# A decoder step with gathered experts: a row's weights and diagonal made on ScalarE instead of VectorE, routing in fifteen parts, queries further ahead

## The chip, the cores and the metric

The kernel runs on one core of a Trainium2 chip. The metric is the device time of one execution in microseconds; the time before is 1787.45 us, the median of three runs (1787.36, 1787.45 and 1790.5).

## The reference, cut to what matters

Two layers work on 288 tokens (256 of a prompt, 32 of a sample group), 1024 wide, all in float32. Each layer has a dense token mixer (a chunked gating MLP in layer 0, a short convolution in layer 1) and then an expert mixer that picks 16 of 16,384 experts for each token and each of 8 heads:

```python
q = (xb @ w_query).reshape(PEER_BLOCK, PEER_HEADS, 2, D_HALF)
s = jnp.einsum('thpd,hpkd->thpk', q, sub_keys)          # scores against 2 x 128 keys
sv, si = lax.top_k(s, TOPK_HALF)                        # 16 best of each half
cand = sv[:, :, 0, :, None] + sv[:, :, 1, None, :]      # 256 sums
cv, ci = lax.top_k(cand.reshape(..., 256), TOPK)        # 16 best sums -> expert indices
...
g = jax.nn.softmax(cv, axis=-1)
u_sel = expert_u[idx]
a = jax.nn.gelu(jnp.einsum('thkd,td->thk', u_sel, xb))  # one number for each picked expert
return jnp.einsum('thk,thkd->td', g * a, expert_v[idx]) # weighted sum of their rows
```

The two expert tables stand side by side in memory, so that one picked expert is one contiguous row of 8 KB: 4 KB of `u` and 4 KB of `v`.

## The kernel before, in words

**Items and turns.** The tokens lie in three tiles: two of 128 prompt tokens and one of the 32 sample tokens, which is spread over 128 partitions with two heads on each quarter. One item is one picked expert for each of the 128 partitions: 128 items for each prompt tile and 32 for the sample tile, so 288 for a layer and 576 in all (`ITEMS`). An item is one gather by GpSimd (L628) of 128 rows, 1.05 MB, into one of eight slots of a ring (`uvring`, `RING = 8`).

The engines run through the items in turns, one item a turn. In turn p VectorE makes the dot product of item p with the tokens (`dot`, L1221). ScalarE makes its gelu (`gelu`, L932). VectorE, in turn p+1 and so after the dot product of item p+1, multiplies gelu, softmax weight and a constant pattern of two stacked identities into a 128x64 block (`weigh`, L1232, written to `diag`; 128x32 for the sample tile, L667 on TensorE). TensorE, also in turn p+1, multiplies that block with the `v` half of the slot and sums it in PSUM (`weigh` of TensorE, L675: 8 instructions for an item). Only then is the slot free: GpSimd waits for TensorE's count `v_tensor` to pass item n-8 before it issues gather n. For the first item of a tile TensorE does items n and n+1 together in turn n+2, since the sum of the tile before has to be read out first.

**The planner.** All other work, the dense mixers, norms, queries, scores and routing of the tile to come, is spread over the same turns by a planner that runs when the kernel is built (`plan_steps`). Each step has an engine, an estimated cost and the steps it needs (`mixer_steps`, `route_steps`). In each turn every engine gets a budget (`ROOM`: in the first tile 1.3 us on VectorE, 2.0 on ScalarE and TensorE) and takes steps in order while its credit lasts. A step may follow one of another engine one turn later, and some two turns after TensorE (`slow`). What is planned for turn -1 (`ahead`) runs before the first item. In each turn an engine first does its part for the item, then its planned steps; TensorE does the planned steps first.

**Routing.** The top-16 search of two heads is nine parts of VectorE steps (`route`, parts 0 to 8). Part 0 finds the best eight scores and their places, part 1 strikes them out and finds the next eight and their places, and so on; part 5 hands the scores to ScalarE's exp, part 8 writes the gather's indices and raises `routed`, for which GpSimd waits. The planner puts parts apart by the turns that are left until they are due (`due`, ten turns before the item), and hurries them where few are left.

**The start.** Turn -1 holds the mixer of tile 0, its queries up to the eighth block, the scores of the first four heads and the routing of the first head. The query weights lie in chunks of 1 MB (two blocks each), some of them in the ring's slots: slot 4 holds the chunk of blocks 8 and 9, slot 7 that of blocks 10 and 11, and a gather into such a slot waits until TensorE has used the chunk (`wait_unused`, in L628's queue).

Of the kernel before, what the change touches and what calls it, by code (L numbers as in the profile page):

```python
# [13 lines left out]
P = 128  # L14
# [105 lines left out]
def mixer_steps(n):  # L120
# [90 lines left out]
    for b in range(HP):  # L211
        out.append(("PE", ("q", n, b), blk, [("xT read", l, "ffn", tiles[-1], 1)]))
        out.append(("ACT", ("q read", n, b), 0.35, [("q", n, b)]))
        for b0, count in scores_of(l, tiles[0]):
            if b0 + count - 1 == b:
# [3 lines left out]
                            [("s", l, tiles[0], b0, count)] + ([("route", *scanned, 1)] if scanned else [])))  # L219
    if 2 in tiles:  # L220
        out.append(("PE", ("s", l, 2, 0, HP), 2.0, [("q read", n, HP - 1)]))
        out.append(("ACT", ("s read", l, 2, 0, HP), 0.6, [("s", l, 2, 0, HP)] + [("route", 0, 2, 0, 1)] * l))
    return out


def route_steps(l, t, i):
    n = dict(calls_of(l, t))[i]
    out = [("DVE", ("route", l, t, i, 0), 0.65 * n, [("s read", *scores_for(l, t, i)[1:])])]
    out += [("DVE", ("route", l, t, i, part), 0.65 * n, []) for part in range(1, 9)]
    out += [("ACT", ("exp", l, t, i), 1.8, [("route", l, t, i, 5)]),  # L230
            ("DVE", ("recip", l, t, i), 0.5, [("exp", l, t, i)])]
    return out
# [17 lines left out]
def group_of(k):  # L250
# [7 lines left out]
    (0, 0): {"DVE": 1.3, "ACT": 2.0, "PE": 2.0},  # L258
# [13 lines left out]
def plan_steps():  # L272
# [7 lines left out]
    cut = [k for _, k, _, _ in first].index(("s read", 0, 0, 4, 4)) + 1  # L280
    ahead = first[:cut] + route_steps(0, 0, 0)
# [34 lines left out]
    while any(q for e in ENGINES for q in queues[e]):  # L316
        room = ROOM[ITEMS[p][:2]] if p < len(ITEMS) else {e: 1000.0 for e in ENGINES}
        for e in ENGINES:
            credit[e] = min(credit[e], 0.0) + room[e]
            plan[e][p] = []  # L320
            while True:
                mine = [q for q in queues[e] if q and ready(e, q[0][1], q[0][3], p)]
                hurry = False
                if e == "DVE" and mine and mine[-1][0][1][0] == "route":
# [17 lines left out]
                if hurry and due(k) - p > 8 - k[4]:  # L342
                    break
# [19 lines left out]
ROUTES = [k[1:4] for k in planned("DVE", ("route",)) if k[4] == 8]  # L363
# [60 lines left out]
def trunk(nc, x_tok, w_chunks, rows, ln_gain, ln_bias, w_s, b_s, conv_w, conv_state, sub_keys,  # L424
          expert_uv, ident_c, iota_c, fold_c, tril_c, smask_c,
          y_tok, v_rows, conv_prompt, conv_sample):
    with ExitStack() as ctx:
# [40 lines left out]
        a_gelu = sb("a_gelu", [P, 2 * TOPK])  # L468
        diag = sb("diag", [P, DIAGS, 64])
# [61 lines left out]
        dotted, gelu_done = sem("dotted"), sem("gelu_done")  # L531
# [102 lines left out]
        def _(pe):  # L634
# [203 lines left out]
            for p in range(-1, TURNS):  # L838
# [4 lines left out]
                for n in (p - 2, p - 1):  # L843
                    if 0 <= n < len(ITEMS) and (n in ITEM0.values()) == (n == p - 2):
# [3 lines left out]
        def _(act):  # L848
# [80 lines left out]
            def gelu(n):  # L929
                act.wait_ge(dotted, n + 1)  # L930
                c = n % (2 * TOPK)
                nc.scalar.activation(a_gelu[:, c:c + 1], a_raw[:, c:c + 1], ACT.Gelu_apprx_tanh).then_inc(gelu_done, 1)  # L932

# [19 lines left out]
            for p in range(TURNS):  # L953
                if p < len(ITEMS):
                    gelu(p)
# [378 lines left out]
```

## Time and profile before

| | |
|---|---|
| median of three runs | 1787.45 us |
| the profiled execution | 1791.12 us, of which the span is 1789.3 us |
| busy in the span | TensorE 1346.1 us, VectorE 1219.4 us, GpSimd 672.8 us, ScalarE 286.5 us |
| moved by DMA | 720.95 MB, 604.02 of them by the 576 gathers; 403 GB/s over the span |
| largest groups | VectorE dot L1221 705.4 us (576 of 1225 ns), TensorE L675 687.2 us, VectorE block L1232 158.9 us (512 of 310 ns), ScalarE gelu L932 116.4 us (576 of 203 ns) |

Engines are called PE (TensorE matmul), PEld (TensorE weight load), DVE (VectorE), ACT (ScalarE), POOL (GpSimd) and SP in the rows. The windows view gives for a stretch of time the busy time of each engine, the granted clock of TensorE as a share of full speed, the mean busy share of the 16 DMA engines, and the rate. In a timeline the bracket behind a row is the idle time of that engine before it and what ended it.

### The profile page before, as it was taken

The numbers are of one execution on the slowest core, as the hardware profiler recorded it, in microseconds if no ns is written. First come the engines' busy times: TensorE is split into PE (matmuls) and PEld (weight loads), VectorE is DVE, ScalarE is ACT, GpSimd is POOL, SyncE is SP. The second block draws the span as 40 slices with busy tenths as digits, with TensorE's granted clock in tenths as the row PEclk, the third lists the DMA queues.
The fourth block names the chain that finished last, engine by engine and source line by source line (L and its number), as shares of the span: only waits on it lengthen the run. The fifth ranks groups of instructions, "written<-read, shape, count | busy, mean of one in ns | idle before, by whom it ended". The sixth has DMA issues, their size and how long they took to land.

```text
span 1789.3 us, 22966 instructions
## 1 busy us (share of the span) xinstructions
PE 1346.1 (75%) x8372; PEld 648.1 (36%) x8372; DVE 1219.4 (68%) x3205; ACT 286.5 (16%) x972; POOL 672.8 (38%) x580
## 2 busy tenths in 40 slices
PE   8987999997896877877664598878786666667643
PEld 7973555542563543541110165324441111111100
DVE  1349867755675766756787876766678877775565
ACT  1112130101122101211021120013112011010011
POOL 0013333234332433434445444434344444444452
PEclk9998999998998998887655599888896766766655
DMA  9949999999999999999999999999999999999995
GB/s 394 387 185 381 384 397 420 421 421 422 421 420 421 418 421 415 411 420 421 419 411 403 398 398 421 422 420 421 421 407 421 413 419 415 411 422 419 421 414 244
DMA packets 101185, 720.95 MB, mean 403 GB/s; under 512 B 12080, under 2 KB 12720, under 8 KB 13872
## 3 DMA queue, kind: packets, MB, share of 16 engines
q0 software_dynamic: 82944, 604.02, 81.9%
q1 hardware_dynamic: 17712, 114.87, 15.6%
q8 instruction: 66, 1.08, 0.2%
q10 hardware_dynamic: 416, 0.60, 0.1%
q14 instruction: 47, 0.39, 0.1%
HBM read 717.93 MB, written 1.52 MB: 402 GB/s over the span
## 4 chain that ended last, share of the span: by engine, by line
DMA 54%; PE 27%; DVE 8%; issue 6%; DVEq 2%; POOL 1%; ACT 0%; SPq 0%; POOLq 0%
DMA uvring<-expert_uv_dram,idx 53%; PE psum L675 10%; PE psum L686 7%; PE psum L804 3%; PE psum L718 3%; DVE uvring L1221 2%; DVE diag L1232 1%; POOL uvring L628 1%; DVEq L1008 1%; DVEq L1016 1%; PE psum L694 1%; PE psum L757 1%; PE psum L667 1%; PE psum L825 1%; DVE ti L1021 1%
## 5 line engine op out<-in xcount | busy, mean ns | idle before, releaser
L628 POOL DMA_INDIRECT uvring<-expert_uv_dram,idx x576 | 672.6, 1168 | 1091.3 <-PE psum L675 836.8
L1221 DVE SCALAR_TENSOR_TENSOR uvring<-uvring,xn 128x1024 f32<-128x1024 f32 x576 | 705.4, 1225 | 446.6 <-DMA uvring<-expert_uv_dram,idx 437.2
L675 PE MATMUL psum<-uvring,diag 64*64 64x512 f32 x4096 | 687.2, 765 | 324.1 <-DVE diag L1232 316.3
L675 PEld LDWEIGHTS psum<-uvring,diag 64*64 64x64 f32 x4096 | 130.6, 154 | 742.8 <-DVE diag L1232 671.7
L932 ACT ACTIVATE a_gelu<-a_raw 128x1 f32<-128x1 f32 x576 | 116.4, 203 | 1348.9 <-DVE uvring L1221 1348.3
L686 PEld LDWEIGHTS psum<-xT,wring 128*128 128x128 f32 x1600 | 216.4, 198 | 72.9 <-issue 64.1
L686 PE MATMUL psum<-xT,wring 128*128 128x160 f32 (+1 forms) x1600 | 236.3, 303 | 3.2 <-DMA wring<-w_chunks_dram 3.2
L1232 DVE TENSOR_SCALAR diag<-twin,a_gelu,gate 128x64 f32<-128x64 f32 x512 | 158.9, 310 | 6.0 <-ACT a_gelu L932 6.0
L667 PE MATMUL psum<-uvring,diag 128*32 128x256 f32 x512 | 68.9, 634 | 92.7 <-DVE diag L1232 87.0
L804 PE MATMUL psum<-wring,arena 128*128 128x256 f32 x288 | 72.0, 407 | 2.6 <-DMA wring<-w_chunks_dram 2.6
L667 PEld LDWEIGHTS psum<-uvring,diag 128*32 128x32 f32 x512 | 13.1, 141 | 150.1 <-DVE diag L1232 140.9
L804 PEld LDWEIGHTS psum<-wring,arena 128*128 128x128 f32 x288 | 57.3, 204 | 23.5 <-issue 9.7
L854 ACT ACTIVATE arena<-psum 128x160 f32<-128x160 f32 (+2 forms) x160 | 45.8, 287 | 84.4 <-PE psum L718 47.9
L686 PEld LDWEIGHTS psum<-xT,kept 128*128 128x128 f32 x320 | 43.3, 202 | 18.2 <-issue 17.4
L686 PE MATMUL psum<-xT,kept 128*128 128x128 f32 (+1 forms) x320 | 47.6, 305 | 0.0
L1221 DVE DVE_READ_ACCUMULATOR uvring<-uvring,xn 128x1 f32 x576 | 47.2, 82 | 0.0
L686 PE MATMUL psum<-xT,uvring 128*128 128x128 f32 x384 | 45.7, 278 | 0.7 <-ACT xT L872 0.7
L686 PEld LDWEIGHTS psum<-xT,uvring 128*128 128x128 f32 x384 | 44.6, 194 | 2.6 <-issue 1.6
L757 PE MATMUL psum<-x,ident 64*128 64x512 f32 x60 | 37.1, 725 | 4.2 <-DMA x<-rows_dram 4.2
L718 PE MATMUL psum<-kept,xT 128*128 128x256 f32 x160 | 39.5, 408 | 0.8 <-ACT xT L872 0.8
L932 ACT ACT_TABLE_LOAD x29 | 37.2, 1283 | 0.5
L718 PEld LDWEIGHTS psum<-kept,xT 128*128 128x128 f32 x160 | 32.4, 206 | 10.0 <-issue 5.2
(116 smaller groups left out, 820.4 us busy)
## 6 DMA issues: line engine op xcount, KB each, us to landing
wring<-w_chunks_dram SPq DMA_DIRECT2D x71, 1024.0 KB, 9.4
uvring<-w_chunks_dram SPq DMA_DIRECT2D x21, 1024.0 KB, 13.3
kept<-w_chunks_dram SPq DMA_DIRECT2D x10, 1024.0 KB, 14.2
uvring<-expert_uv_dram,idx POOLq DMA_INDIRECT x576, 14.5
x<-x_tok_dram SPq DMA_DIRECT2D x2, 512.0 KB, 4.1
uvring<-ln_gain_dram SPq DMA_DIRECT2D x1, 1024.0 KB, 28.9
uvring<-ln_bias_dram SPq DMA_DIRECT2D x1, 1024.0 KB, 29.3
keys<-sub_keys_dram SPq DMA_DIRECT2D x2, 512.0 KB, 16.9
```

The source lines that it names most:

```text
L628: pool.indirect_dma_start(uvring[:, n % RING, :], None, expert_uv, bass.IndirectOffsetOnAxis(ap=idx[t][:, i:i + 1], axis=0),).then_inc(uv_ ...
L667: mm = nc.tensor.matmul(acc[32 * q:32 * q + 32, 0:256], diag[:, n % DIAGS, 0:32], row[:, D + 256 * q:D + 256 * (q + 1)], start=first, stop ...
L675: mm = nc.tensor.matmul(acc[64 * j:64 * j + 64, 512 * i:512 * (i + 1)], diag[64 * i:64 * i + 64, n % DIAGS, :], row[64 * i:64 * i + 64, D ...
L686: mm = nc.tensor.matmul(bank(key, WIDTH[n]), w[:, k, j * P:(j + 1) * P], act[:, k, 0:cols], start=(k == 0), stop=(k == KD - 1))
L694: mm = nc.tensor.matmul(psum[f:f + 32, b0:b0 + WCOLS], act[:, kk, :], w[:, kk, :], start=start and kk % 2 == 0, stop=stop and kk % 2 == 1)
L718: mm = nc.tensor.matmul(bank(k, WCOLS, ROWS[t]), xT[:, kk, LCOL[t]:LCOL[t] + ROWS[t]], w[:, kk, :], start=(kk == 0), stop=(kk == KD - 1))
L757: nc.tensor.matmul(bank(k), matrix, values, start=True, stop=True).then_inc(group_done, 1)
L804: mm = nc.tensor.matmul(bank(key, WCOLS, ROWS[t]), act[:, h * KD + kk, LCOL[t]:LCOL[t] + ROWS[t]], w[:, kk, :], start=(h == 0 and kk == 0) ...
L854: nc.scalar.activation(out, bank(key, n, rows), func).then_inc(scalar_read, 1)
L932: nc.scalar.activation(a_gelu[:, c:c + 1], a_raw[:, c:c + 1], ACT.Gelu_apprx_tanh).then_inc(gelu_done, 1)
L1221: nc.vector.scalar_tensor_tensor(out=uvring[:, slot, 0:D], in0=uvring[:, slot, 0:D], scalar=1.0, in1=xn[t][:, :], op0=ALU.mult, op1=ALU.mu ...
L1232: nc.vector.tensor_scalar(diag[:, n % DIAGS, 0:32 if t == 2 else 64], fold[:, :] if t == 2 else twin[:, :], a_gelu[:, c:c + 1], gate[t][:, ...
```

## The change

- **Weights and diagonal on ScalarE.** VectorE's `weigh` is gone. ScalarE's `gelu` becomes `weigh`: the gelu, then a multiply with the softmax weight into a new 128x32 tile `wgt`, then a multiply of the constant pattern with that number into `diag`, each waiting for the one before it, and for the softmax weights of the head (`normalised`) at its first item.
- **The same turn.** TensorE takes item p in turn p instead of p+1, and the first two items of a tile in turn n+1 instead of n+2.
- **Routing in fifteen parts.** The same VectorE instructions are cut at their drains into fifteen parts, with a planned cost for each; planned costs for two heads add up to 17.3 us instead of 11.7. The spacing of the parts and what may be hurried in one turn follow new formulas.
- **Queries further ahead.** Turn -1 now goes on to query block 11 and the scores of the next two heads; the exp of the first head comes right after the copy of query block 6.
- The budget of TensorE in the first tile is 1.9 instead of 2.0 us a turn, and the residual add may follow TensorE one turn later instead of two.

```diff
-                            [("s", l, tiles[0], b0, count)] + ([("route", *scanned, 1)] if scanned else [])))
+                            [("s", l, tiles[0], b0, count)] + ([("route", *scanned, SCANNED)] if scanned else [])))
...
+PARTS = [0.45, 0.65, 0.65, 0.45, 0.65, 0.5, 0.4, 0.5, 0.5, 0.4, 0.5, 0.6, 0.7, 0.7, 1.0]
+SCANNED, SCORED, PICKED = 4, 11, len(PARTS) - 1
...
-    out = [("DVE", ("route", l, t, i, 0), 0.65 * n, [("s read", *scores_for(l, t, i)[1:])])]
-    out += [("DVE", ("route", l, t, i, part), 0.65 * n, []) for part in range(1, 9)]
+    out = [("DVE", ("route", l, t, i, part), cost * n, [] if part else [("s read", *scores_for(l, t, i)[1:])])
+           for part, cost in enumerate(PARTS)]
...
-    (0, 0): {"DVE": 1.3, "ACT": 2.0, "PE": 2.0},
+    (0, 0): {"DVE": 1.3, "ACT": 2.0, "PE": 1.9},
...
-    cut = [k for _, k, _, _ in first].index(("s read", 0, 0, 4, 4)) + 1
-    ahead = first[:cut] + route_steps(0, 0, 0)
+    cut = [k for _, k, _, _ in first].index(("s read", 0, 0, 8, 4)) + 1
+    ahead = first[:cut]
+    at = [k for _, k, _, _ in ahead].index(("q read", 0, 6)) + 1
+    ahead[at:at] = route_steps(0, 0, 0)
...
-        slow = 2 if k[0] in ("v read", "vq read", "u read", "bch read", "q read", "gate", "add") else 1
+        slow = 2 if k[0] in ("v read", "vq read", "u read", "bch read", "q read", "gate") else 1
...
-                    gap = (due(k) - 6 - p) // (9 - k[4])
-                    hurry = gap < 2
-                    if p < routed_at + min(gap, 3):
+                    gap = (due(k) - 3 - p) / (PICKED + 1 - k[4])
+                    hurry = gap < 1.5
+                    if p < routed_at + min(int(gap), 2):
...
-                if hurry and due(k) - p > 8 - k[4]:
+                hurried += hurry
+                if hurry and hurried * max(due(k) - p, 1) > PICKED - k[4]:
                     break
...
-                for n in (p - 2, p - 1):
-                    if 0 <= n < len(ITEMS) and (n in ITEM0.values()) == (n == p - 2):
+                for n in (p - 1, p):
+                    if 0 <= n < len(ITEMS) and (n in ITEM0.values()) == (n == p - 1):
                         weigh(n)
...
-            def gelu(n):
+            def weigh(n):
+                _, t, i = ITEMS[n]
+                c = n % (2 * TOPK)
                 act.wait_ge(dotted, n + 1)
                 nc.scalar.activation(a_gelu[:, c:c + 1], a_raw[:, c:c + 1], ACT.Gelu_apprx_tanh).then_inc(gelu_done, 1)
...
+                act.wait_ge(gelu_done, n + 1)
+                nc.scalar.mul(wgt[:, c:c + 1], a_gelu[:, c:c + 1], gate[t][:, i:i + 1]).then_inc(weighed, 1)
+                if n >= DIAGS:
+                    act.wait_ge(v_tensor, n - DIAGS + 1)
+                act.wait_ge(weighed, n + 1)
+                nc.scalar.mul(diag[:, n % DIAGS, 0:32 if t == 2 else 64], fold[:, :] if t == 2 else twin[:, :],
+                              wgt[:, c:c + 1]).then_inc(diag_ready, 1)
...
-            def weigh(n):
-                dve.wait_ge(gelu_done, n + 1)
-                if n >= DIAGS:
-                    dve.wait_ge(v_tensor, n - DIAGS + 1)
-                nc.vector.tensor_scalar(diag[:, n % DIAGS, 0:32 if t == 2 else 64],
-                                        fold[:, :] if t == 2 else twin[:, :], a_gelu[:, c:c + 1],
-                                        gate[t][:, i:i + 1], ALU.mult, ALU.mult).then_inc(diag_ready, 1)
...
                 if p < len(ITEMS):
                     dot(p)
-                if 1 <= p <= len(ITEMS):
-                    weigh(p - 1)
```

## Rows read from the trace of the kernel before

**Rows 1.** The page: DMA in 40 slices (tenths, then GB/s), and the chain's shares.
```profile
DMA  9949999999999999999999999999999999999995
GB/s 394 387 185 381 384 397 420 421 421 422 421 420 421 418 421 415 411 420 421 419 411 403 398 398 421 422 420 421 421 407 421 413 419 415 411 422 419 421 414 244
DMA 54%; PE 27%; DVE 8%; issue 6%; DVEq 2%; POOL 1%; ACT 0%; SPq 0%; POOLq 0%
```

**Rows 2.** Windows: stretch, its length, engines' busy us (instructions), PEclk, DMA share, GB/s.
```profile
143.00:147.00 4.00, 4.00 (x36) 1.84 (x36) 3.77 (x11) 2.13 (x7) 2.45 (x2) 1.00 0.21 45
...
200.00:240.00 40.00, 40.00 (x295) 21.58 (x294) 24.28 (x63) 10.46 (x31) 13.81 (x14) 1.00 0.92 352
240.00:600.00 360.00, 308.65 (x2059) 177.88 (x2058) 243.03 (x619) 61.60 (x204) 124.74 (x112) 0.93 1.01 421
600.00:800.00 200.00, 154.51 (x1064) 90.05 (x1060) 132.69 (x367) 28.66 (x111) 72.31 (x62) 0.90 1.01 417
...
880.00:960.00 80.00, 45.50 (x256) 7.82 (x248) 64.67 (x168) 13.29 (x42) 38.72 (x32) 0.59 1.00 404
...
1010.00:1050.00 40.00, 34.65 (x232) 18.68 (x232) 35.87 (x101) 11.49 (x34) 16.16 (x14) 0.83 0.96 371
...
1300.00:1600.00 300.00, 200.76 (x1066) 46.85 (x1064) 235.54 (x618) 45.44 (x160) 133.42 (x118) 0.73 1.01 415
1600.00:1760.00 160.00, 94.59 (x508) 15.50 (x504) 98.00 (x204) 16.70 (x68) 76.90 (x63) 0.60 1.01 418
...
1769.00:1778.00 9.00, 3.88 (x32) 0.60 (x24) 4.34 (x9) 0.61 (x3) 0.00 (x0) 0.50 0.14 56
```

**Rows 3.** Timeline of all engines, 134 to 145 us: start, duration, engine, line.
```profile
134.78 1.23 DVE L1221 SCALAR_TENSOR_TENSOR uvring<-uvring,xn 128x1024 f32<-128x1024 f32 x1
...
136.30 1.98 PE L675 MATMUL psum<-uvring,diag 64*64 64x512 f32 x8 [5.24 <-DVE diag L1232]
...
141.26 2.72 PE L686 MATMUL psum<-xT,uvring 128*128 128x128 f32 x16
...
144.25 1.92 POOL L628 DMA_INDIRECT uvring<-expert_uv_dram,idx  x1 [11.00 <-PE psum L686]
```

**Rows 4.** Timeline, 1625 to 1632 us: one item's way from its landing to the next gather.
```profile
1625.29 1.23 DVE L1221 SCALAR_TENSOR_TENSOR uvring<-uvring,xn 128x1024 f32<-128x1024 f32 x1 [1.02 <-DMA uvring<-expert_uv_dram,idx]
...
1626.55 0.20 ACT L932 ACTIVATE a_gelu<-a_raw 128x1 f32<-128x1 f32 x1 [2.28 <-DVE uvring L1221]
...
1628.92 0.31 DVE L1232 TENSOR_SCALAR diag<-twin,a_gelu,gate 128x64 f32<-128x64 f32 x1
...
1629.29 1.86 PE L675 MATMUL psum<-uvring,diag 64*64 64x512 f32 x8 [0.50 <-DVE diag L1232]
...
1631.46 0.94 POOL L628 DMA_INDIRECT uvring<-expert_uv_dram,idx  x1 [1.42 <-PE psum L675]
```

**Rows 5.** Groups of ScalarE by line and form: count, busy us, mean ns, idle before.
```profile
L932 ACT ACTIVATE a_gelu<-a_raw 128x1 f32<-128x1 f32 x576 | 116.4, 203 | 1348.9 <-DVE uvring L1221 1348.3
L932 ACT ACT_TABLE_LOAD x29 | 37.2, 1283 | 0.5
L926 ACT ACT_TABLE_LOAD x19 | 24.4, 1283 | 0.3
...
L854 ACT ACTIVATE arena<-psum 128x128 f32<-128x128 f32 x72 | 19.0, 265 | 34.7 <-PE psum L686 34.7
L861 ACT ACT_TABLE_LOAD x14 | 18.0, 1283 | 1.6 <-PEq L1320 1.3
L907 ACT COPY scores<-psum 128x512 f32<-128x512 f32 x17 | 9.5, 572 | 1.3 <-PE psum L825 1.3
```

**Rows 6.** Timeline of POOL: three gathers in the stretches named.
```profile
216.03 0.98 POOL L628 DMA_INDIRECT uvring<-expert_uv_dram,idx  x1 [5.69 <-PE psum L675]
...
1020.75 1.29 POOL L628 DMA_INDIRECT uvring<-expert_uv_dram,idx  x1 [3.85 <-PE psum L675]
...
1762.62 1.64 POOL L628 DMA_INDIRECT uvring<-expert_uv_dram,idx  x1 [0.85 <-PE psum L667]
```

More of the change, by code:

```diff
@@ L319, in plan_steps @@
             credit[e] = min(credit[e], 0.0) + room[e]
-            plan[e][p] = []
+            plan[e][p], hurried = [], 0
             while True:
@@ L468, in trunk @@
         a_gelu = sb("a_gelu", [P, 2 * TOPK])
+        wgt = sb("wgt", [P, 2 * TOPK])
         diag = sb("diag", [P, DIAGS, 64])
@@ L954, in _ @@
                 if p < len(ITEMS):
-                    gelu(p)
+                    weigh(p)
                 for lt, end in LAST.items():
@@ L1008, in first8, with replace @@
                     dve.drain()
-                    for values, best, where in lists:
-                        V.max_index(where[:, 0:8], best[:, 0:8], values)
-                    dve.drain()
-                def next8(lists, signal=None):
+                def replace(lists):
                     for values, best, _ in lists:
@@ L1016, in next8, with second @@
                     dve.drain()
+                def second(lists):
                     for values, best, _ in lists:
@@ L1019, in next8, with places @@
                     dve.drain()
+                def places(lists, at):
                     for values, best, where in lists:
-                        V.max_index(where[:, 8:16], best[:, 8:16], values)
-                    done = dve.drain()
-                    if signal:
-                        done.then_inc(signal, 1)
+                        V.max_index(where[:, at:at + 8], best[:, at:at + 8], values)
+                    return dve.drain()
                 if part == 0:
                     dve.wait_ge(scalar_read, G[scores_for(l, t, i)][3])
-                    first8(sides)
+                    first(sides)
                 elif part == 1:
-                    next8(sides, scanned)
+                    places(sides, 0)
                 elif part == 2:
+                    replace(sides)
+                elif part == 3:
+                    second(sides)
+                elif part == SCANNED:
+                    places(sides, 8).then_inc(scanned, 1)
+                elif part == 5:
                     V.tensor_copy(tif[:, 0:2 * H, :], ti[:, 0:2 * H, :])
@@ L1037, in route @@
                     dve.drain()
-                elif part == 3:
-                    first8(both)
-                elif part == 4:
-                    next8(both)
-                elif part == 5:
+                elif part == 6:
+                    first(both)
+                elif part == 7:
+                    places(both, 0)
+                elif part == 8:
+                    replace(both)
+                elif part == 9:
+                    second(both)
+                elif part == 10:
+                    places(both, 8)
+                elif part == SCORED:
                     V.tensor_tensor(gate[t][:, c].rearrange("p (a b) -> p a b", b=TOPK), cv[:, 0:H, :],
@@ L1050, in route @@
                     dve.drain()
-                elif part == 6:
+                elif part == 12:
                     V.tensor_tensor(pick[:, 0:2 * H * TOPK, :],
@@ L1260, in _ @@
             dve.wait_ge(const_landed, 16 * N_CONST)
-            after(did(nc.vector.tensor_tensor(twin[:, :], ident[:, 0:64], ident[:, 64:P], ALU.add)))
+            nc.vector.tensor_tensor(twin[:, :], ident[:, 0:64], ident[:, 64:P], ALU.add).then_inc(twin_ready, 1)
             for p in range(TURNS):
```

30 lines of the change are left out of this document (16 added, 14 removed).

## The prediction

> **What bounds the kernel now.** I read the DMA slices first. From the eighth slice on they stand at 420 to 422 GB/s wherever nothing disturbs them, and the whole stretch from 240 to 600 us averages 421 at a DMA share of 1.01, while TensorE is busy 86% and VectorE 68% of it [rows 1, 2]. So 421 GB/s is the ceiling, and the chain agrees: 54% of it is DMA [rows 1]. Work that only makes an engine's day shorter buys nothing there. What can be bought is the time in which DMA runs below the ceiling. For each stretch that is length x (1 - rate / 421) [rows 2]:
>
> 143 to 147 us: 4 x (1 - 45/421) = 3.6 us. 200 to 240: 40 x (1 - 352/421) = 6.6. 600 to 800: 1.9. 880 to 960: 3.2. 1010 to 1050: 4.8. 1300 to 1600: 4.3. 1600 to 1760: 1.1. Together 25.5 us; the start before the first gather (the third slice) and the drain at the end are not touched by the change.
>
> Then I asked in each hole who was late. At 143 us [rows 3]: gather 7 went out at 144.25 after 11.0 us of waiting for TensorE's query blocks 10 and 11 (L686), whose chunk lay in its slot. TensorE reached the last of them only at 141.26, because in its queue the first rows came before it and it had waited 5.24 us for a diagonal; that diagonal came after the second dot product, which VectorE began only at 134.78 behind four parts of routing. In 200 to 240 us TensorE is busy 40.0 of 40 us, and GpSimd waited 5.69 us for a row [rows 2, 6]. In 1010 to 1050 VectorE is busy 35.9 of 40, and GpSimd waited 3.85 us for a row [rows 2, 6]; 880 to 960 is of the same kind, with VectorE at 81%.
>
> **The row's way.** One row's way, undisturbed, stands in the pure stretch near the end [rows 4]. The dot product starts at landing, 1625.29. Gelu is done at 1626.75. The block is made only after the next dot product, 1628.92 to 1629.23; TensorE then takes 1.86 us, and the gather into the slot starts at 1631.46: 6.2 us from landing to gather. After the change: dot product until about 1626.5 (gelu started at 1626.55), gelu 0.20, two multiplies, TensorE 1.86, and the 0.3 us from TensorE's end to the gather that the rows show. The trace has no ScalarE multiply by a per-row factor. From below it is the 128x1 gelu, 203 ns; from above, for a 128x64 block, the 128x128 form of 265 ns, unless the multiply forced a change of tables, 1283 ns each [rows 5]. I exclude that: there are 29 loads at L932 for 576 gelus, and 19 and 14 at exp and root, although the copies of L854 and L907 run between the gelus [rows 5]. I take 0.20 + 0.23, and three hand-overs of 0.05 (1626.55 against 1626.5 is one). So TensorE starts at 1626.55 + 0.20 + 0.43 + 0.15 = 1627.3 and the gather at 1629.5, 4.2 us after landing; with the upper end 4.3. **Each slot comes back about 1.9 us earlier**, in holes and outside. VectorE loses 0.31 us of each turn and the wait for it, 159 us in all (the block's own row in the table of the profile).
>
> The Trainium skill (ScalarE: Activation LUTs, Rules for kernel authors) says to put multiplies on VectorE and not on ScalarE; its cost section (What ACT_TABLE_LOAD costs) adds about 93 ns for a per-partition operand, by which I estimate 0.28 and 0.33 us for the two multiplies and a way of 4.4 us instead of 4.2. The mean of 203 ns for a gelu with fixed factors is near its formula. By the rule the change would be wrong; what it would cost here is the first rival.
>
> **Part by part.** *Queries ahead.* Blocks 8 to 11 run straight on from about 125 us, at most 2.72 us each [rows 3], so the first gather into slot 7 goes out by 136 instead of 144.25, and the first row is taken near 139: ScalarE must first copy the scores of the next heads. Eight gathers of 2.49 us (1.049 MB at 421 GB/s) from about 125 us last until 145, so gather 8 comes in time. The hole of 3.6 us goes whole. The first exp before block 7's copy costs that copy some 0.2 us, hidden by GpSimd's gathers 0 to 3.
>
> *200 to 240 us.* Work on TensorE is not less, but its budget a turn is 5% less (1.9 for 2.0), the dense work starts four turns sooner, and the 1.9 us keep one more gather in flight while TensorE is late. Bounds: nothing, and all of 6.6; I take 4.0.
>
> *880 to 960 and 1010 to 1050.* VectorE is the late one. Of a turn of 2.49 us it gets 0.31 back, and the longest piece of routing between two dot products shrinks to about a third (nine parts into fifteen, the longest of them cut in three). At the change of tile ScalarE's table load for root now holds a row back, which takes some of it away. Bounds 0 and 8.0; I take 5.0 (2.0 and 3.0).
>
> *600 to 800 and 1300 to 1760.* Single bursts. At the end of the run, 1769 to 1778, the share is 0.14 of 16 engines: one or two DMA engines work on for some 8 us after the others [rows 2]. A hole of a few tenths of a microsecond is filled for the others only, and these set the landing. So of 7.3 us I take 1.9 (0.6 and 1.3); bounds 0 and 7.3.
>
> *Drain.* The last row has two multiplies more in its chain and VectorE's block less: 0.43 + 0.1 - 0.31, and the copies behind it as late: I take 0.5 lost; bounds 0.2 and 0.6.
>
> *No effect:* the earlier residual add, the new costs and the parts' spacing outside the holes, since DMA is at its ceiling. ScalarE gets 576 x 0.43 = 248 us more on its 286: it stays under a third.
>
> Sum: 3.6 + 4.0 + 5.0 + 1.9 - 0.5 = **14.0 us**. The profiled execution took 1791.1 us, so it would be 1777.1; it lay 3.7 above the median, so I predict **1773.5 us** for the median. The bounds put it between 1787.45 - 3.6 + 0.6 = 1784.5 and 1787.45 - 25.5 + 0.2 = 1762.
>
> **Rivals.** *ScalarE's queue sets the slots free later (slower).* Place: the turns with an exp or a root. A table load, two exps (about 0.8) and the load back to gelu hold ScalarE for 1.28 + 0.8 + 1.28 = 3.4 us [rows 5], and now the next row stands behind them; before, gelu stood there and VectorE's block came a turn later. It decides when a slot's spare is under 3.4 us: the last gather's issue ended at 1764.26 and most DMA engines went idle near 1769 [rows 6, 2], so a gather was issued 4.8 us, less its own 2.5, ahead of need: 2.3, and 1.9 more by the change: 4.2. If the spare is smaller elsewhere and each of the 33 changes [rows 5] costs 0.4 us, that is 13 us with only the first hole won: 1787.45 - 3.6 + 13 = 1797. Against it: 4.2 is over 3.4. Chance 0.08.
>
> *The slowest DMA engine already sets the pace.* Then holes of the mean rate are not holes of that engine, except the first, where the share fell to 0.21. Result 1784.5, give or take 2. For it: the tail just named. Against it: at 352 GB/s over 40 us 16% of the sixteen engines' time is missing, more than two of them could hide. Chance 0.17. The Trainium skill (DMA: Bandwidth & Descriptors, Latency and other measured facts) states that two of the 16 engines are usually slower than the rest; the 0.14 agrees with that in number, and nothing here shows which they are.
>
> *All holes close:* 1762. For it: every hole is a late slot, and every slot comes 1.9 us sooner. Against it: TensorE's 40.0 of 40 us. Chance 0.13.
>
> *The plan brings holes elsewhere,* for instance where fifteen parts are hurried before the second tile, and gives most back: 1786. VectorE's instructions are the same, so I see no reason for it: 0.04.
>
> **From the cases to the numbers.** The forecast, 1767 to 1781, has 0.58. A difference of 0.2%, 3.6 us, is about what a measurement of this kernel tells from none. Faster by more: 0.58 + 0.13 + under half of the second rival, 0.07 = 0.78; within: 0.10 + 0.04 = 0.14; slower: 0.08. The range, 1761 to 1786, leaves out the slower rival, an edge of the others, and some 0.1 for what I do not see.
>
> **What would show it.** Right: no window below 300 GB/s between 126 and 200 us; a gather 4.2 to 4.6 us after a landing in the pure stretches; no table load at the multiplies and 33 or so changes as before; 200 to 240 us (some ten us earlier) over 380 GB/s, 1010 to 1050 over 400; the same 421 GB/s at best. Wrong: GpSimd's waits for TensorE longest right behind exps (first rival), or holes closed and the end not earlier (second).

## The result, and the profile after

The kernel after takes 1777.48 us (median of 5 runs, 1774.24 to 1779.77) against 1788.42 for the kernel before in the same comparison (5 runs, 1787.36 to 1790.5): ratio 0.9934, 95% interval 0.9923 to 0.9945, so 10.9 us faster. Forecast were 1773.5 us, in a range of 1761 to 1786. Its profiled execution took 1777.48 us, span 1775.7; that of before 1791.12, span 1789.3.

The page of the kernel after: the 40 slices of VectorE, ScalarE and the DMA, then the chain's shares.

```profile
DVE  1348577555664666555676775676567766666454
ACT  1114443234342423433443442326343433434343
DMA  9949999999999999999999999999999999999996
GB/s 391 389 181 421 379 416 420 421 421 421 420 421 421 420 421 421 419 419 421 419 413 418 405 422 420 421 421 417 421 413 408 417 422 421 421 421 420 420 402 255
DMA 53%; PE 32%; ACT 6%; DVE 5%; issue 2%; POOL 1%; DVEq 0%; ACTq 0%; SPq 0%; POOLq 0%
```

The ceiling is the same as in [rows 1], 420 to 422 GB/s; the slices that had 381 to 411 outside the start mostly stand closer to it. The windows of after answer to [rows 2] (stretch, length, busy us and instructions of PE, PEld, DVE, ACT and POOL, PEclk, DMA share, GB/s):

```profile
143.00:147.00 4.00, 4.00 (x36) 2.53 (x36) 2.53 (x4) 2.11 (x5) 2.26 (x2) 1.00 1.00 412
190.00:240.00 50.00, 45.60 (x320) 25.24 (x322) 29.47 (x81) 22.75 (x66) 16.57 (x16) 0.97 0.96 379
200.00:240.00 40.00, 35.60 (x244) 20.16 (x248) 21.59 (x56) 15.37 (x45) 13.23 (x14) 0.96 0.97 385
240.00:600.00 360.00, 305.72 (x2046) 176.78 (x2038) 218.87 (x516) 135.06 (x440) 137.56 (x116) 0.91 1.01 421
600.00:800.00 200.00, 157.73 (x1055) 91.38 (x1053) 117.55 (x292) 68.55 (x236) 73.21 (x63) 0.88 1.01 420
880.00:960.00 80.00, 42.44 (x256) 7.63 (x256) 57.28 (x136) 33.06 (x107) 33.96 (x32) 0.59 1.01 415
1010.00:1050.00 40.00, 40.00 (x292) 24.96 (x285) 30.75 (x76) 20.47 (x71) 20.32 (x17) 0.96 0.99 409
1300.00:1600.00 300.00, 206.83 (x1063) 47.73 (x1066) 204.83 (x490) 117.92 (x391) 123.25 (x118) 0.70 1.01 418
1600.00:1760.00 160.00, 90.56 (x512) 15.72 (x504) 88.70 (x157) 59.37 (x200) 60.46 (x59) 0.59 0.99 409
```

143 to 147 us went from 45 to 412 GB/s, 200 to 240 from 352 to 385, 1010 to 1050 from 371 to 409 with VectorE at 30.75 us where it had 35.87. The hole at 200 us starts ten us sooner now; over 190 to 240 us the rate is 379, and before it was 366:

```profile
190.00:240.00 50.00, 50.00 (x357) 28.00 (x355) 33.60 (x96) 11.80 (x37) 17.41 (x17) 1.00 0.94 366
```

The 409 of 1600 to 1760 us takes in the end of the stream, which comes sooner than before, and a hole behind a change of tile (356 from 1690 to 1700 us).

Since the work has moved in time, I also measured by rows (a row is one item, numbered from 0): for each whole 1 us window 1 - rate / 421, added up between the starts of the dot products of given rows. This "lost stream" is 76.5 us for before and 62.3 for after. Both kernels move the same bytes, so the difference, 14.2, has to be that of the spans, 13.6, but for the last part of a microsecond: lost stream tells where time was lost, not why.

One row's way, answering to [rows 4]:

```profile
1682.15 1.23 DVE L1258 SCALAR_TENSOR_TENSOR uvring<-uvring,xn 128x1024 f32<-128x1024 f32 x1 [1.25 <-DMA uvring<-expert_uv_dram,idx]
...
1683.42 0.20 ACT L945 ACTIVATE a_gelu<-a_raw 128x1 f32<-128x1 f32 x1 [1.51 <-DVE uvring L1258]
1683.65 0.29 ACT L953 ACTIVATE wgt<-a_gelu,gate 128x1 f32<-128x1 f32 x1
1684.04 0.35 ACT L957 ACTIVATE diag<-twin,wgt 128x64 f32<-128x64 f32 x1
...
1684.44 1.76 PE L686 MATMUL psum<-uvring,diag 64*64 64x512 f32 x8 [0.50 <-ACT diag L957]
...
1686.52 0.94 POOL L639 DMA_INDIRECT uvring<-expert_uv_dram,idx  x1 [1.34 <-PE psum L686]
```

From landing to the next gather it takes 4.4 us, where it took 6.2. ScalarE's groups, answering to [rows 5]:

```profile
L957 ACT ACTIVATE diag<-twin,wgt 128x64 f32<-128x64 f32 x512 | 178.1, 348 | 47.7 <-ACT wgt L953 1.1
L953 ACT ACTIVATE wgt<-a_gelu,gate 128x1 f32<-128x1 f32 x576 | 169.7, 295 | 20.9
L945 ACT ACTIVATE a_gelu<-a_raw 128x1 f32<-128x1 f32 x576 | 116.4, 202 | 882.6 <-DVE uvring L1258 882.1
L945 ACT ACT_TABLE_LOAD x29 | 37.2, 1283 | 0.5
```

29 table loads at the gelu, as before: the multiplies bring none.

### The profile page after: what moved, and what is told of

It is laid out like the page before. It is cut to its first block, busy times and chain, and to the rows that moved or that the text cites. A ratio compares the mean times of both kernels' runs of the same rounds, so it can differ in the third digit from the quotient of the medians.

```text
span 1775.7 us, 23560 instructions
## 1 busy us (share of the span) xinstructions
PE 1343.0 (76%) x8372; PEld 651.2 (37%) x8372; DVE 1084.2 (61%) x2629; ACT 652.3 (37%) x2124; POOL 640.4 (36%) x580
## 4 chain that ended last, share of the span: by engine, by line
DMA 53%; PE 32%; ACT 6%; DVE 5%; issue 2%; POOL 1%; DVEq 0%; ACTq 0%; SPq 0%; POOLq 0%
DMA uvring<-expert_uv_dram,idx 52%; PE psum L686 11%; PE psum L697 10%; DVE uvring L1258 4%; PE psum L815 4%; PE psum L729 3%; POOL uvring L639 1%; ACT diag L957 1%; ACT wgt L953 1%; DMA wring<-w_chunks_dram 1%; ACT a_gelu L945 1%; ACT L945 1%; PE psum L836 1%; PE psum L705 1%; PE psum L719 1%
## 5 line engine op out<-in xcount | busy, mean ns | idle before, releaser
L639 POOL DMA_INDIRECT uvring<-expert_uv_dram,idx x576 | 640.2, 1111 | 1108.6 <-PE psum L686 859.7
L697 PEld LDWEIGHTS psum<-xT,wring 128*128 128x128 f32 x1600 | 219.2, 200 | 76.5 <-issue 66.0
L957 ACT ACTIVATE diag<-twin,wgt 128x64 f32<-128x64 f32 x512 | 178.1, 348 | 47.7 <-ACT wgt L953 1.1
L953 ACT ACTIVATE wgt<-a_gelu,gate 128x1 f32<-128x1 f32 x576 | 169.7, 295 | 20.9
L678 PEld LDWEIGHTS psum<-uvring,diag 128*32 128x32 f32 x512 | 13.3, 142 | 149.2 <-ACT diag L957 135.1
L697 PEld LDWEIGHTS psum<-xT,kept 128*128 128x128 f32 x320 | 45.0, 210 | 18.2 <-issue 16.6
L1048 DVE FIND_INDEX8 ti<-tv,scores 128x8 uint32<-128x128 f32 x144 | 38.4, 285 | 0.0
## 6 DMA issues: line engine op xcount, KB each, us to landing
uvring<-w_chunks_dram SPq DMA_DIRECT2D x21, 1024.0 KB, 13.6
keys<-sub_keys_dram SPq DMA_DIRECT2D x2, 512.0 KB, 16.6
```

The lines of the kernel that those rows point to most:

```text
L639: pool.indirect_dma_start(uvring[:, n % RING, :], None, expert_uv, bass.IndirectOffsetOnAxis(ap=idx[t][:, i:i + 1], axis=0),).then_inc(uv_ ...
L678: mm = nc.tensor.matmul(acc[32 * q:32 * q + 32, 0:256], diag[:, n % DIAGS, 0:32], row[:, D + 256 * q:D + 256 * (q + 1)], start=first, stop ...
L697: mm = nc.tensor.matmul(bank(key, WIDTH[n]), w[:, k, j * P:(j + 1) * P], act[:, k, 0:cols], start=(k == 0), stop=(k == KD - 1))
L953: nc.scalar.mul(wgt[:, c:c + 1], a_gelu[:, c:c + 1], gate[t][:, i:i + 1]).then_inc(weighed, 1)
L957: nc.scalar.mul(diag[:, n % DIAGS, 0:32 if t == 2 else 64], fold[:, :] if t == 2 else twin[:, :], wgt[:, c:c + 1]).then_inc(diag_ready, 1)
L1048: V.max_index(where[:, at:at + 8], best[:, at:at + 8], values)
```

## The experiments

In the diffs, lines that only carry names, semaphores or the sample tile's form are left out. Three numbers of each run's trace stand beside its time: the mean time from the start of a row's dot product to the start of the gather into its slot (568 pairs of the two timelines; "way"); VectorE's idle time before dot products, ended by a gather's landing ("VectorE waits"); and the lost stream of rows 0 to 16, 16 to 48 and 48 to 560, in us. All ratios are to the kernel before in the same comparison, 5 runs of each kernel or more. The kernel after, e1 to e4, e5 to e8, e9 to e11 and e12 were measured at different times, so across these groups the ratios count.

| run | us, median | ratio, 95% | way | VectorE waits | 0-16 | 16-48 | 48-560 |
|---|---|---|---|---|---|---|---|
| before | 1787.7 to 1789.3 | 1 | 7.34 | 437 | 4.5 | 6.5 | 15.6 |
| after | 1777.48 | 0.9934 [0.9923, 0.9945] | 5.59 | 543 | 0.0 | 4.9 | 8.7 |
| e1 ScalarE's part alone | 1780.56 | 0.9955 [0.9942, 0.9969] | 5.43 | 542 | 6.7 | 2.3 | 7.0 |
| e2 queries ahead alone | 1787.33 | 0.9993 [0.9984, 1.0002] | 7.23 | 434 | 0.0 | 7.8 | 13.8 |
| e3 all but ScalarE's part | 1788.35 | 0.9996 [0.9987, 1.0005] | 7.24 | 438 | 0.1 | 8.8 | 14.6 |
| e4 block on VectorE, same turn | 1792.27 | 1.0016 [1.0007, 1.0026] | 4.75 | 190 | 2.8 | 8.3 | 16.6 |
| e5 TensorE a turn later | 1776.91 | 0.9933 [0.9919, 0.9946] | 6.26 | 551 | 0.0 | 7.4 | 7.8 |
| e6 ScalarE's part and queries | 1776.08 | 0.9933 [0.9920, 0.9947] | 5.47 | 514 | 0.0 | 3.6 | 6.6 |
| e7 earlier read-out of the sum | 1776.23 | 0.9932 [0.9918, 0.9945] | 5.54 | 540 | 0.0 | 6.7 | 6.1 |
| e8 early multiply | 1775.07 | 0.9927 [0.9913, 0.9940] | 5.11 | 545 | 0.0 | 3.2 | 7.0 |
| e9 block on ScalarE, a row later | 1778.10 | 0.9938 [0.9924, 0.9952] | 8.08 | 559 | 0.0 | 7.3 | 7.5 |
| e10 VectorE makes a spare block | 1786.55 | 0.9987 [0.9978, 0.9996] | 5.45 | 414 | 0.1 | 6.9 | 15.6 |
| e11 e6 and early multiply | 1774.50 | 0.9924 [0.9911, 0.9938] | 5.26 | 516 | 0.0 | 2.2 | 7.9 |
| e12 e11 and earlier read-out | 1774.74 | 0.9920 [0.9906, 0.9933] | 5.20 | 513 | 0.6 | 3.7 | 5.1 |

**Taking the change apart.** e1 is the kernel before with this part alone:

```diff
-                dve.wait_ge(gelu_done, n + 1)
-                nc.vector.tensor_scalar(diag[...], twin[:, :], a_gelu[...], gate[...], ALU.mult, ALU.mult)
+                nc.scalar.mul(wgt[:, c:c + 1], a_gelu[:, c:c + 1], gate[t][:, i:i + 1])
+                nc.scalar.mul(diag[...], twin[:, :], wgt[:, c:c + 1])
-                for n in (p - 2, p - 1):
+                for n in (p - 1, p):
```

> The kernel before with one part of the change: ScalarE makes the row's weights and block, and TensorE takes the row in the same turn; queries and routing stay as they were (nine parts). Theory A (a slot comes back about 1.8 us earlier, and the holes of the gathers' stream after the first one close): the first hole at 143 to 147 us stays (4.1 us of lost stream, as before), the holes between 200 and 1050 us close as in the kernel after, so about 1788.4 - 9.5 = 1779 us (1776 to 1783). Rival B (the gain is the finer routing and the smoother VectorE queue): no more than the 113 us that VectorE no longer spends on blocks helps, 1784 to 1787. Rival C (the transfers are paced by the slowest DMA engine, and only the first hole counts): 1788 us, no change.

e2 is the kernel before with the queries ahead alone (its first line here; the routing of the first head moves with it), e3 the whole change without the lines of e1:

```diff
-    cut = [k for _, k, _, _ in first].index(("s read", 0, 0, 4, 4)) + 1
+    cut = [k for _, k, _, _ in first].index(("s read", 0, 0, 8, 4)) + 1
```

> The kernel before with one part of the change: the queries and scores of eight heads, in place of four, are done ahead of the first turn; the rest as before (nine parts, VectorE makes the block, TensorE takes the row one turn later). Theory A: only the first hole goes, 1788.4 - 4 = 1784.5 us (1783 to 1787), all later holes as before. Rival B: as A here, since the routing keeps its nine parts. Rival C (only the first hole counts, and it is worth more than its 4 us of lost stream): 1778 to 1781 us.

> The whole change but for the part on ScalarE: queries of eight heads ahead, routing in fifteen parts, and the planner's two small numbers with it; VectorE makes the block and TensorE takes the row one turn later, as in the kernel before. Theory A: the first hole goes, and of the others only what long routing parts on VectorE caused, 1788.4 - 4 - 1 = 1783.5 us (1781 to 1786). Rival B (finer routing is what closes the holes): 1777 to 1780 us, as the kernel after. Rival C: as the queries alone.

ScalarE's part alone is worth 8.0 us (0.45% of 1788.4); the queries alone 1.3 (interval from 2.9 gained to 0.4 lost), with the finer routing beside them 0.7 (from 2.3 gained to 0.9 lost). Theory A gave e2 1784.5 and e3 1783.5 us, and both lie above its ranges. Rival B (finer routing) falls with e3, C (only the first hole counts) with e1. In e2's trace the first hole is gone, and its next stretch loses 7.8 us of stream where it lost 6.5.

e4 keeps the block on VectorE but puts it right behind the row's own dot product, and leaves the rest as after:

```diff
                 if p < len(ITEMS):
                     dot(p)
-                if 1 <= p <= len(ITEMS):
-                    weigh(p - 1)
+                if p < len(ITEMS):
+                    weigh(p)
```

> The whole change, but VectorE makes the block, now in the same turn right behind its dot product (it waits there for ScalarE's gelu), and TensorE takes the row in that turn as in the kernel after. The slot's way back is as short as in the kernel after or shorter (one multiply of 0.2 us in place of two of 0.3), but VectorE stands still for some 0.8 us a row and keeps the 113 us of blocks. Theory A (what counts is how early the slot comes back): 1777 to 1782 us, a part of it given back where VectorE is full of routing. Rival B (what counts is VectorE's relief): 1785 to 1795 us, since VectorE has 0.8 us less in each turn of 2.5. Rival C: as the queries alone, 1784 us.

This was the surprise. The way is the shortest of all, 4.75 us, and the kernel is slower than before. Its VectorE groups (count, busy us, mean ns, idle before and its releasers):

```profile
L1241 DVE SCALAR_TENSOR_TENSOR uvring<-uvring,xn 128x1024 f32<-128x1024 f32 x576 | 705.1, 1224 | 207.8 <-DMA uvring<-expert_uv_dram,idx 190.0 <-issue 0.4
L1252 DVE TENSOR_SCALAR diag<-twin,a_gelu,gate 128x64 f32<-128x64 f32 x512 | 199.7, 390 | 170.1 <-ACT a_gelu L941 170.1
```

VectorE now stands still 170.1 us for the gelus of these rows, and the block takes 390 ns where it took 310. Its dot products find a landed row more often: 199 of 576 wait for a landing, 369 before, and they wait 190 us in all, not 437. Theory A, an early slot is what counts, can't give 1792 us.

The way leaves out how long a landed row lies before its dot product. With that counted in, from the landings that the traces give to the gather into the slot, e4 still holds a slot for less time than the kernel before, 6.1 us in the mean against 7.8 (504 of the 576 landings of before are in its trace), and is slower.

**The way against VectorE's time.** e5 gives TensorE its rows a turn later, as before, and leaves the block on ScalarE:

```diff
-                for n in (p - 1, p):
+                for n in (p - 2, p - 1):
```

> The kernel after with one thing undone: TensorE takes the row one turn later, as in the kernel before; ScalarE still makes weights and block, so VectorE stays relieved of 113 us. The way from the start of a row's dot product to the gather into its slot was 5.6 us in the mean in the kernel after and 7.3 before; here it should be about 7.5 again. Theory A' (what counts is the whole way from landing to the free slot, VectorE's lateness before the dot and the rest behind it alike): a good half of the gain goes, 1783 to 1788 us. Rival B (only VectorE's relief counts, as the run with the block kept on VectorE in the same turn suggests): 1777 to 1780 us, as the kernel after, whatever the way.

1776.91 us, as after: rival B. But the way grew only to 6.26 us and not to the 7.5 that the run was to give, since TensorE reaches the row's turn as soon as it has no dense work. Two further runs separate the two causes. e9 leaves the block on ScalarE and makes it late, behind the next row's gelu, as VectorE did; with e5's edit. e10 is the kernel after with a block on VectorE that nobody reads (the remarks in the two diffs are mine):

```diff
+                if 1 <= p <= len(ITEMS):       # ScalarE, behind the gelu of row p
+                    block(p - 1)
```

```diff
+                if 1 <= p <= len(ITEMS):       # VectorE, behind the dot product of row p
+                    weigh(p - 1)               # into spare[:, 0:64]
```

> The kernel after, but ScalarE makes a row's block in the order in which VectorE made it in the kernel before: behind the gelu of the next row, so that it waits for the next row's dot product, and TensorE takes it one turn later. VectorE stays relieved. The way from a dot product to the gather into its slot should be as long as in the kernel before, 7.3 us in the mean (6.2 in the steady stretches; 5.6 and 4.5 in the kernel after). Theory V (VectorE's time is what counts: 0.39 us a row of blocks gone, whatever the way): 1776 to 1780 us, as the kernel after. Theory W (the way is what counts, as the prediction had it): 1784 to 1789 us. If each has a part: between, 1780 to 1784.

> The kernel after, and VectorE makes the block once more, at the place where the kernel before makes it (behind the next row's dot product), into a spare tile that nobody reads: some 0.2 to 0.4 us of VectorE in each of 576 rows, with the way of the row as short as in the kernel after. Theory V: the gain goes, 1784 to 1790 us. Theory W: 1776 to 1780 us, as the kernel after, since nobody waits for the spare block. If each has a part: between.

e9's timeline shows the long way in a steady stretch, row landed at 1640.98:

```profile
1640.98 1.23 DVE L1265 SCALAR_TENSOR_TENSOR uvring<-uvring,xn 128x1024 f32<-128x1024 f32 x1 [1.24 <-DMA uvring<-expert_uv_dram,idx]
...
1642.24 0.20 ACT L945 ACTIVATE a_gelu<-a_raw 128x1 f32<-128x1 f32 x1 [1.65 <-DVE uvring L1265]
...
1644.83 0.28 ACT L958 ACTIVATE wgt<-a_gelu,gate 128x1 f32<-128x1 f32 x1
...
1645.20 0.35 ACT L962 ACTIVATE diag<-twin,wgt 128x64 f32<-128x64 f32 x1
...
1645.60 1.99 PE L686 MATMUL psum<-uvring,diag 64*64 64x512 f32 x8 [1.39 <-ACT diag L962]
...
1647.89 0.94 POOL L639 DMA_INDIRECT uvring<-expert_uv_dram,idx  x1 [2.40 <-PE psum L686]
```

6.9 us from landing to gather, longer than the 6.2 of before, 8.08 in the mean against 7.34; and 1778.10 us, the time of the kernel after. In e10 the way is as short as after, 5.45, and the time is 1786.55: all but 1.8 us of the gain is gone. Its VectorE groups:

```profile
L1260 DVE SCALAR_TENSOR_TENSOR uvring<-uvring,xn 128x1024 f32<-128x1024 f32 x576 | 705.8, 1225 | 424.7 <-DMA uvring<-expert_uv_dram,idx 413.6 <-issue 1.3
L1273 DVE TENSOR_SCALAR spare<-twin,a_gelu,gate 128x64 f32<-128x64 f32 x512 | 159.3, 311 | 13.5 <-ACT a_gelu L946 13.5
```

So theory V holds: 576 blocks on VectorE, 178 us in all (159 and 19 for the sample tile) and 14 us of waits for gelus, cost some 9 us of the end (1786.55 against 1777.48; 0.9987 against 0.9934). The 2.5 us that e9's way is longer than after's cost nothing that can be told (intervals 0.9924 to 0.9952 and 0.9923 to 0.9945), nor are e3 and e10 told apart, which both have VectorE's blocks and ways of 7.24 and 5.45 us (0.9996 and 0.9987, intervals that overlap). The intervals leave room for some 3 us of the way's own. Counted from the landing, as for e4, e10 holds a slot for 5.9 us and e9 for 8.3, and e9 is the faster one.

The last column of the table agrees: 14 to 17 us lost between rows 48 and 560 wherever VectorE makes blocks, with ways from 4.75 to 7.34 us, and 5 to 9 where it doesn't, with ways from 5.11 to 8.08.

It is not that GpSimd issues its gathers more slowly beside VectorE's blocks: one takes 1100 ns in the mean in e10 and 1111 in the kernel after, and the stream runs at 421 GB/s from 280 to 600 us in e10 too.

The 113 us that the expectations of e1, e4 and e5 name for the blocks, and the 0.39 us a row of e9's, are not what the trace of before shows: 158.9 + 19.0 = 178 us, 0.31 a row.

How VectorE makes a hole is seen in the kernel before at 1012 to 1031 us, in its own timeline (all its dot products, and at 1040.85 the next one that waits; what lies between is left out):

```profile
1012.18 1.20 DVE L1221 SCALAR_TENSOR_TENSOR uvring<-uvring,xn 128x1024 f32<-128x1024 f32 x1
...
1016.95 1.22 DVE L1221 SCALAR_TENSOR_TENSOR uvring<-uvring,xn 128x1024 f32<-128x1024 f32 x1
...
1020.02 1.21 DVE L1221 SCALAR_TENSOR_TENSOR uvring<-uvring,xn 128x1024 f32<-128x1024 f32 x1
...
1022.71 1.21 DVE L1221 SCALAR_TENSOR_TENSOR uvring<-uvring,xn 128x1024 f32<-128x1024 f32 x1
...
1025.00 1.22 DVE L1221 SCALAR_TENSOR_TENSOR uvring<-uvring,xn 128x1024 f32<-128x1024 f32 x1
...
1026.38 1.22 DVE L1221 SCALAR_TENSOR_TENSOR uvring<-uvring,xn 128x1024 f32<-128x1024 f32 x1
...
1027.75 1.22 DVE L1221 SCALAR_TENSOR_TENSOR uvring<-uvring,xn 128x1024 f32<-128x1024 f32 x1
...
1030.90 1.23 DVE L1221 SCALAR_TENSOR_TENSOR uvring<-uvring,xn 128x1024 f32<-128x1024 f32 x1
...
1040.85 1.23 DVE L1221 SCALAR_TENSOR_TENSOR uvring<-uvring,xn 128x1024 f32<-128x1024 f32 x1 [0.26 <-DMA uvring<-expert_uv_dram,idx]
```

Until 1040.85 no row has a wait in brackets: every gather had landed before VectorE came to it. With norms, blocks and routing between them, the first four dot products start 4.77, 3.07 and 2.69 us apart, and the stream wants one each 2.49 us; slots come back at VectorE's pace, not the DMA's. Then VectorE catches up, down to 1.37 us from one to the next. Twelve rows in a row (290 to 301) find their data landed. In the kernel after these are seven (290 to 296), and from 1018.57 on dot products wait for landings again:

```profile
1018.57 1.22 DVE L1258 SCALAR_TENSOR_TENSOR uvring<-uvring,xn 128x1024 f32<-128x1024 f32 x1 [0.84 <-DMA uvring<-expert_uv_dram,idx]
...
1023.54 1.23 DVE L1258 SCALAR_TENSOR_TENSOR uvring<-uvring,xn 128x1024 f32<-128x1024 f32 x1 [1.25 <-DMA uvring<-expert_uv_dram,idx]
```

The windows of 1010 to 1050 us put the two runs in the order of their times, e9 first, then e10:

```profile
1010.00:1050.00 40.00, 39.71 (x286) 24.51 (x287) 30.49 (x72) 18.55 (x70) 19.58 (x17) 0.95 0.99 400
```

```profile
1010.00:1050.00 40.00, 37.44 (x265) 20.96 (x257) 34.74 (x87) 22.63 (x71) 19.45 (x17) 0.93 0.97 385
```

**What could still be gained.** e6 is the change with the routing left in nine parts, without the fifteen:

```diff
-    out = [("DVE", ("route", l, t, i, part), cost * n, ...) for part, cost in enumerate(PARTS)]
+    out += [("DVE", ("route", l, t, i, part), 0.65 * n, []) for part in range(1, 9)]
```

> The change without the finer routing: ScalarE's part and the queries ahead, routing in nine parts as before. The part on ScalarE alone lost 6.7 us of stream at the start and 2.3 us in TensorE's dense stretch up to 280 us, the whole change none and 4.9; behind that the part on ScalarE alone lost 7.0 us and the whole change 8.7. Theory A' (the fifteen parts bring nothing of their own once rows come back early, they are only the means to fit the queries): 1775 to 1779 us, as the kernel after or a little under. Rival B (VectorE's short parts matter): 1779 to 1783 us.

The fifteen parts bring nothing of their own that can be told: 0.9933 against 0.9934. On top of ScalarE's part the queries do seem to pay: 0.9955 in e1, 0.9933 here, 3.9 us, though the two intervals just meet and e6 has the planner's two small numbers of the change as well.

e7 reads the sum out a turn earlier and frees the accumulator for TensorE once it is read:

```diff
-                    if p == end + 2:
+                    if p == end + 1:
...
-                    pe.wait_ge(acc_read, list(LAST).index((l, t)))
+                    pe.wait_ge(acc_turned, list(LAST).index((l, t)))
+                    pe.wait_ge(acc_seen, list(LAST).index((l, t)))
```

> The kernel after, and the sum of a tile is read out one turn earlier (VectorE and ScalarE at the first turn of the next tile, not the second), and TensorE may start the next tile's sum when the accumulator has been read, not only when its last third has been added. In the kernel after the two first rows of a tile wait for this (TensorE 5.1 us at 1691 us), and the stretches around the five changes of tile behind the first one lost some 1.3 + 1.5 + 2.0 + 2.0 us of stream. Theory A': 2 to 5 us less than after, 1773 to 1775.5. Rival B (the holes at the tiles come from VectorE's steps there, the norm and the sum, not from the held slots): 1776 to 1779.

e8 multiplies gate and pattern before the dot product is waited for:

```diff
+                nc.scalar.mul(pre[:, n % 2, 0:w], twin[:, :], gate[t][:, i:i + 1])
                 act.wait_ge(dotted, n + 1)
                 nc.scalar.activation(a_gelu[...], a_raw[...], ACT.Gelu_apprx_tanh)
-                nc.scalar.mul(wgt[:, c:c + 1], a_gelu[:, c:c + 1], gate[t][:, i:i + 1])
-                nc.scalar.mul(diag[...], twin[:, :], wgt[:, c:c + 1])
+                nc.scalar.mul(diag[...], pre[:, n % 2, 0:w], a_gelu[:, c:c + 1])
```

> The kernel after, with the two multiplies reordered: gate times pattern is made before the dot product is waited for, so that only gelu and one multiply stand between dot and block. The way is 0.3 to 0.4 us shorter in each of 576 rows, VectorE's work is the same, ScalarE's about the same (one 0.35 us multiply in place of a 0.30 us one). Theory A' (lateness anywhere on the way counts, but only where a hole is left): 0 to 2 us less, 1775.5 to 1777.5. Rival B (VectorE alone): 1777 to 1778, no change. A third (each 0.1 us of the way counts in every row): it would be 5.6 us per 1.8 us of way and so about 2 us less.

e11 is e6 with e8's edit, e12 is e11 with e7's edit:

> Two runs that were at or a little under the kernel after, in one: ScalarE's part and the queries ahead with routing in nine parts (1776.1), and the multiply of gate and pattern made before the dot product is waited for (1775.1). Theory V (the way of a row counts for nothing, VectorE's work is the same): 1775 to 1777.5 us. Theory W (each tenth of a us of the way counts): 1773 to 1775.5 us.

> The run before (ScalarE's part, queries ahead, nine parts, early multiply; 1774.5 us) with the earlier read-out of a tile's sum added. VectorE's work is the same but for the turn in which it adds the sum. Theory V (VectorE's time counts, not the waits of rows for the accumulator): 1773.5 to 1776 us, no change that can be told. Rival (the changes of tile are what is left: that run lost 1.2 + 4.9 us of stream between rows 256 and 304, the one with the earlier read-out alone 1.9): 1770 to 1773 us.

e7 gave 0.9932, e8 0.9927, e11 1774.50 us (0.9924), e12 1774.74 (0.9920). Each beats the kernel before; none is told from the kernel after, whose interval overlaps all four. e11 lies in the range of theory W and just under that of V, and e8 lies under both of its ranges. By the ratios the early multiply takes 1.3 us off the kernel after and 1.6 off e6, each time within the intervals, so a small worth of the way is not excluded. e7's lost stream between rows 48 and 560 is smaller than after's, 6.1 against 8.7, but its time does not show it.

## Why the prediction was right, and where its reason was wrong

The time lies in the range and 4.0 us above the forecast. The step that failed is the one in bold: "Each slot comes back about 1.9 us earlier". It does (4.4 us against 6.2), but e9 and e10 show that this is not what closes holes. The gain I put beside it in half a sentence, that VectorE loses 0.31 us of each turn, accounts for most of the gain (the 159 us given with it leave out the 19 of the sample tile). Eight slots of 2.49 us are 19.9 us; with a way of 6.9 in e9 13 us are left for the transfer itself, and e9 still runs at the ceiling in its long stretch:

```profile
240.00:600.00 360.00, 311.55 (x2039) 178.74 (x2039) 219.53 (x515) 122.49 (x438) 129.25 (x116) 0.90 1.01 421
```

Point by point, in lost stream of the two profiled executions:

- First hole, forecast 3.6 us: rows 0 to 16 lost 4.5 and lose none, and the first dot product comes 0.5 us of stream later. The mechanism was right, but its worth shows only together with ScalarE's part: 3.9 us between e1 and e6, 1.3 alone, not told from none. Why e2 gives most of it back is not settled; its next stretch loses 1.3 us more.
- 200 to 240 us, forecast 4.0: 1.6 (rows 16 to 48, 6.5 to 4.9). The hole starts ten us sooner, as forecast, but in 190 to 230 us the rate is 376 and not over 380. This term was mis-sized, and by the failed step: the mean way in these rows is 13.3 us after and 13.1 before, so slots came back no earlier here. The timeline of the kernel after shows why:

```profile
216.84 0.35 ACT L957 ACTIVATE diag<-twin,wgt 128x64 f32<-128x64 f32 x1
...
217.81 3.72 PE L729 MATMUL psum<-wring,xT 128*128 128x256 f32 x16 [1.25 <-DMA wring<-w_chunks_dram]
...
221.57 0.38 ACT L865 ACTIVATE arena<-psum 128x256 f32<-128x256 f32 x1 [4.39 <-PE psum L729]
...
222.86 0.93 POOL L639 DMA_INDIRECT uvring<-expert_uv_dram,idx  x1 [5.63 <-PE psum L686]
...
227.56 3.89 PE L697 MATMUL psum<-xT,wring 128*128 128x160 f32 x16 [3.15 <-DMA wring<-w_chunks_dram]
...
231.38 2.98 PE L686 MATMUL psum<-uvring,diag 64*64 64x512 f32 x24
231.48 0.31 ACT L865 ACTIVATE arena<-psum 128x160 f32<-128x160 f32 x1 [3.72 <-PE psum L697]
...
232.95 0.94 POOL L639 DMA_INDIRECT uvring<-expert_uv_dram,idx  x1 [7.92 <-PE psum L686]
```

  The block made at 216.84 is taken by TensorE only at 231.38, behind its dense work and two waits for weight chunks, and GpSimd waits 7.92 us for it. In rows 16 to 48 a finished block waits 6.4 us in the mean for TensorE, much as before (6.8). The block itself comes no sooner either, 5.1 us after the dot product's start against 4.7 before (from row 48 on 2.4 against 4.3): ScalarE's queue, the gelu in it, stands behind copies that wait until TensorE's dense work ends. In the old plan the same move does shorten the way here, from 13.1 us to 10.3 in e1; the fifteen parts lengthen it, from 11.3 in e6 to 13.3 in after and, with the two small numbers, from 12.7 in e2 to 14.0 in e3. The prediction counted no such effect of the parts. How much of the lost stream is due to which stays open: the runs with the block on ScalarE lose 2.2 to 7.4 us here, and after, e7 and e8, with nearly one plan, 3.2 to 6.7.
- 880 to 960 and 1010 to 1050 us, forecast 2.0 and 3.0: 1.8 and 3.3 (rows 224 to 272 and 272 to 320). Here the reason given, a late VectorE, was the right one.
- 600 to 800 and 1300 to 1760 us, forecast 1.9: 1.7 (rows 48 to 224) and 0.1 (rows 320 to 560).
- Drain, forecast 0.5 lost: the end from row 560 on lost 1.7 us of stream less, 16.8 against 18.5; the other traces show 16.3 to 18.8 there, so this is no more than their spread.
- That the sum comes out so near is luck in part: 2.4 us too many at 200 to 240 are made up by 0.9 more at the first hole and by an end that lost 1.7 us less where 0.5 more was forecast.
- The multiplies, 0.20 + 0.23 us: 295 and 348 ns, both above the upper end I gave, 265. The Trainium skill (ScalarE: Activation LUTs, What ACT_TABLE_LOAD costs), by which I estimated 0.28 and 0.33, agrees with the trace within 6%, and its way of 4.4 us is the measured one. The rule of the same page of the Trainium skill to put multiplies on VectorE (Rules for kernel authors) makes this kernel slower: e3, with the blocks on VectorE, stands at 0.9996 where the kernel after stands at 0.9934, though each block takes 310 ns there and 643 in two multiplies here.
- The miss of 4.0 us: executions compared with executions, 14.0 were forecast and 13.6 measured; medians fell by 10.9. I took the holes of one execution and then only shifted its level by 3.7. But that execution, 1791.12 us, was longer than every run of before that stands beside an experiment (at most 1790.83), so a part of the holes I counted probably belongs to that execution and not to the kernel; no second trace of before was taken.

Rivals: the slowest DMA engine does not set the pace. By that rival only the first hole counts, and e1, which keeps that hole (6.7 us lost in rows 0 to 16), gains 8.0 us. ScalarE's queue sets no slots free so late that it costs the gain: a way longer still, in e9, costs nothing that can be told. The plan brings no new holes that give the gain back. Not all holes close: rows 16 to 560 still lose 13.6 us of 22.1.

## What to carry to other kernels

When a stream is fed through a ring of buffers, ask first which engine in the ring is late in the stretch. If the first instruction for a buffer no longer waits for the transfer, the work in that engine's queue sets the pace there; the latency behind it was free here as long as ring length times period covered it together with the transfer. Two runs that cross the two causes (same latency with the work put back, same work with the latency put back) settle what a change that does both is worth; a shorter chain by itself proved nothing here. And take the size of holes from more than one execution before subtracting them from a median.

## What was not expected of the hardware

Where an instruction stands in an in-order queue has a price beside its work: in e4 the same block on VectorE, placed where it waits for ScalarE's gelu, made the kernel 3.9 us slower than e3, where it stands a row later and waits 8 us in all instead of 191. That is still less than the 9 us that the blocks themselves cost in e10. And 8.1 us of way (e9) against 5.6 (after) cost nothing that can be told at 421 GB/s with eight slots.
